# Gate weights in two passes, an own wait for the first x tile, and a changed order in a GLA/MLA/ConvGLU step

## The reference

```
h = rmsnorm(x, norm_mix[0])
q, k, v, r = split(h @ w_in)
log_a = log_sigmoid((h @ w_a1) @ w_a2 + b_a) / 16      # w_a1: 1024 x 16, w_a2: 16 x 512
b = cumsum(log_a) within a chunk
scores = sum_d q_i k_j exp(b_i - b_j), causal;  o = scores @ v + (q exp(b)) @ S
S_new = exp(b_last) S + (k exp(b_last - b))^T @ v       # S: the recurrent state, 128 x 256
o = rmsnorm(o) * silu(r);  x = x + o @ w_out
```

## Time and profile before

| | us |
|---|---|
| median of 3 runs | 2765.77 |
| lowest, highest | 2765.39, 2768.36 |
| profiled execution, its own time | 2768.41 |
| its span | 2766.6 |
| PE busy | 2708.2 (98%) |
| DVE busy | 1146.8 (41%) |
| ACT busy | 900.4 (33%) |
| POOL busy | 769.3 (28%) |

### The profile page before, as it was taken

One profiled execution on the slowest core, in us unless ns is written; L12 is line 12 of the kernel. 1 busy time (PEld: TensorE's weight loads), 2 busy tenths in 40 slices (PEclk: granted clock), 3 DMA queues, 4 the chain that ended last, 5 costly groups with the idle time before them and its releaser, 6 DMA issues.

```text
span 2766.6 us, 41263 instructions
## 1 busy us (share of the span) xinstructions
PE 2708.2 (98%) x17210; PEld 2607.8 (94%) x17210; DVE 1146.8 (41%) x2182; ACT 900.4 (33%) x1605; POOL 769.3 (28%) x324
## 2 busy tenths in 40 slices
PE   8999999999999999999999999999999999999999
PEld 6899999999999999999988888888999999999998
DVE  6634344463333333333624336556733333333324
ACT  7333242451111111112546666444521111111121
POOL 4121221262222222223512113322432222222221
PEclk9999999999999999999999999999999999999999
DMA  3110101011111111111213352212011111111112
GB/s 105 36 37 31 48 20 49 20 46 46 47 46 46 46 46 46 46 46 46 72 58 110 113 197 96 82 52 70 16 46 46 46 46 46 46 46 46 46 47 80
DMA packets 156507, 156.81 MB, mean 57 GB/s; under 512 B 15122, under 2 KB 137632, under 8 KB 156208
## 3 DMA queue, kind: packets, MB, share of 16 engines
q1 hardware_dynamic: 153935, 152.20, 17.2%
q10 hardware_dynamic: 2400, 2.10, 0.2%
HBM read 128.12 MB, written 26.15 MB: 56 GB/s over the span
## 4 chain that ended last, share of the span: by engine, by line
PE 90%; DVE 5%; ACT 2%; issue 2%; DMA 1%; SPq 0%; POOL 0%; DVEq 0%; ACTq 0%; POOLq 0%
PE ps L303 25%; PE ps L305 24%; PE ps L304 24%; PE ps L1864 2%; PE ps L852 2%; PE ps L1577 2%; PE ps L839 1%; PE ps L1848 1%; PE ps L840 1%; PE ps L841 1%; DVE xT L530 1%; DVE aP L2007 1%; DVE fa L716 1%; PE ps L923 1%; ACT aP L1950 1%
## 5 line engine op out<-in xcount | busy, mean ns | idle before, releaser
L303 PE MATMUL ps<-hh,whi 128*128 128x352 f32 x2664 | 864.5, 325 | 0.7 <-DVE hl L437 0.4
L304 PE MATMUL ps<-hl,whi 128*128 128x352 f32 x2664 | 854.8, 321 | 0.0
L305 PE MATMUL ps<-hh,wlo 128*128 128x352 f32 x2664 | 854.5, 321 | 0.0
L268 POOL TENSOR_TENSOR wlo<-wraw,whi 128x2048 fp32r<-128x2048 f32 (+1 forms) x79 | 361.5, 4575 | 660.9 <-ACT whi L261 631.6
L303 PEld LDWEIGHTS ps<-hh,whi 128*128 128x128 f32 x2664 | 500.6, 188 | 3.6 <-issue 1.3
L304 PEld LDWEIGHTS ps<-hl,whi 128*128 128x128 f32 x2664 | 501.3, 188 | 1.1 <-issue 0.2
L305 PEld LDWEIGHTS ps<-hh,wlo 128*128 128x128 f32 x2664 | 499.8, 188 | 0.0
L530 DVE TENSOR_TENSOR xT<-xT,ps 128x352 f32<-128x352 f32 x720 | 371.8, 520 | 261.9 <-PE ps L305 260.8
L303 PE MATMUL ps<-fahi,whi 128*128 128x352 f32 x1056 | 343.2, 325 | 2.6
L261 ACT ACTIVATE whi<-wraw 128x2048 fp32r<-128x2048 f32 x82 | 157.1, 1916 | 579.1 <-DMA wraw<-w_ffn_in 458.2
L305 PE MATMUL ps<-fahi,wlo 128*128 128x352 f32 x1056 | 341.2, 323 | 0.0
(11 more groups left out here) (301 smaller groups left out, 4091.4 us busy)
## 6 DMA issues: line engine op xcount, KB each, us to landing
wraw<-w_ffn_in SPq DMA_DIRECT2D x88, 512.0 KB, 4.9
wraw<-w_ffn_out SPq DMA_DIRECT2D x44, 512.0 KB, 4.1
wraw<-w_gla_in SPq DMA_DIRECT2D x24, 512.0 KB, 4.5
s_k<-kw SPq DMA_DIRECT2D x8, 784.0 KB, 3.3
akraw<-s_k SPq DMA_DIRECT2D x8, 784.0 KB, 4.2
s_v<-vst SPq DMA_DIRECT2D x8, 768.0 KB, 4.4
av<-s_v SPq DMA_DIRECT2D x8, 768.0 KB, 4.1
aqraw<-s_q SPq DMA_DIRECT2D x8, 528.0 KB, 5.8
```

The costliest lines, as they stand in the source:

```text
L268: pool.tensor_tensor(lo[:, 0:cols], raw[:, 0:cols], hi[:, 0:cols].bitcast(F32), ALU.subtract).then_inc(S("w_lo"), 1)
L303: nc.tensor.matmul(out, w[0], x[0], start=start, stop=False)
L304: nc.tensor.matmul(out, w[0], x[1], start=False, stop=False)
L305: return nc.tensor.matmul(out, w[1], x[0], start=False, stop=stop)
```

## The change

- The first x tile (tile 0) counts on the semaphore `consts`, together with the identity and the ones matrix. TensorE waits for it alone, then for tiles 1 and 2, then for 3 to 5, then for 6 to 8.
- TensorE turns tiles 4 and 5 behind the sums of chunk 0 instead of ahead of them.
- The gate weights w_a1 lie in one tile `a1p` of 48 columns per row tile: hi, zeros, lo. Per row tile there are two matmuls instead of three: all 48 columns by the hi activations, 16 columns by the lo ones. The part from lo weights comes out on partitions 32 to 47; ACT copies it to a sixth used block of `zs` (now 112 partitions), and `zah` gets a fourth copy of w_a2.
- At the first head, v unit 0 waits for 8 of the 12 minima; the other 4 are waited for behind it. ACT's last q/k copy comes ahead of the first decays. DVE does the minima of chunk 2 ahead of a scan. POOL clears `gkd` instead of DVE, for head 0.
- POOL splits the chunk for r (`gc(h, 2)`) in eight pieces of 256 columns instead of four of 512, in all heads.
- The output products wait for each state where it is first read, instead of for all nine ahead of the first.

```diff
@@ split_parts, pe_gla_t
-        def split_parts(who, c, parts=range(4)):
+        def split_parts(who, c, parts=range(4), n_parts=4):
...
-                cols = slice(q * WC // 4, (q + 1) * WC // 4)
+                cols = slice(q * WC // n_parts, (q + 1) * WC // n_parts)
...
-            wv = views((a1hi, a1lo), 0, KD, GRANK)
             for k in range(KD):
                 row_ready(pe, 0, j, k)
-                last = mm3(ps[0:GRANK, B_BANKS[j], 0:TC], [v[:, k, :] for v in wv],
-                           (hh[:, k, tc(j)], hl[:, k, tc(j)]), k == 0, k == KD - 1)
+                if k:
+                    pe.matmul(ps[0:GRANK, B_BANKS[j], 0:TC], a1p[:, k, 0:GRANK], hl[:, k, tc(j)], start=False, stop=False)
+                last = pe.matmul(ps[0:3 * GRANK, B_BANKS[j], 0:TC], a1p[:, k, :], hh[:, k, tc(j)],
+                                 start=(k == 0), stop=(k == KD - 1))
+                if k == 0:
+                    pe.matmul(ps[0:GRANK, B_BANKS[j], 0:TC], a1p[:, k, 0:GRANK], hl[:, k, tc(j)], start=False, stop=False)
             last.then_inc(S("t_mm"), 1)
@@ pe_gla_head
-                    pe.wait_ge(S("z_min"), NCH * GH)
+                    pe.wait_ge(S("z_min"), 2 * GH)
...
             pe.wait_ge(S("qk_sb"), h * 6 + 6)
+            pe.wait_ge(S("z_min"), NCH * GH)
...
-            pe.wait_ge(S("state"), h * 9 + 9)
             pe.wait_ge(S("qb"), h + 1)
...
                     if g > 0:
+                        if r_ < 3:
+                            pe.wait_ge(S("state"), h * 9 + g)
@@ t_copy (ACT)
-                for r_ in (0, 4):
-                    last = act.activation(zs[r_ * GRANK:(r_ + 1) * GRANK, tc(j)], ps[0:GRANK, B_BANKS[j], 0:TC], ACT.Copy)
+                for r_ in (0, 4, 6):
+                    t0 = 2 * GRANK if r_ == 6 else 0
+                    last = act.activation(zs[r_ * GRANK:(r_ + 1) * GRANK, tc(j)], ps[t0:t0 + GRANK, B_BANKS[j], 0:TC], ACT.Copy)
@@ act_gla_start
+            act_gla_qk(act, 6, 1, 2)
             act_gla_decays(act, 0, 0)
-            act_gla_qk(act, 6, 1, 2)
@@ dve_gla
-            z_scan(1, 0)
             for h in range(GH):
                 z_min(2, h)
+            z_scan(1, 0)
...
-            dve.wait_ge(S("z_log"), NCH * GH)
-            dve.memset(gkd[:, :], 0.0).then_inc(S("kd_zero"), 1)
@@ pool_gla_head, pool_gla
-            split_parts(pool, gc(h, 2))
+            split_parts(pool, gc(h, 2), range(8), 8)
...
             pool_split(pool, gc(0, 1), WC)
+            pool.wait_ge(S("z_log"), NCH * GH)
+            pool.memset(gkd[:, :], 0.0).then_inc(S("kd_zero"), 1)
@@ tensor: x_turn and the order
-                if t % 3 == 0:
-                    pe.wait_ge(S(f"x_loaded{t // 3}"), 3 * 16)
+                if t in (0, 1, 3, 6):
+                    pe.wait_ge(S(x_loaded(t)), 3 * 16 if t != 1 else 2 * 16)
...
-            for t in range(6):
+            for t in range(4):
                 x_turn(t)
             pe.wait_ge(S("mix_loaded"), 16)
             pe.transpose(ps[:, 3, 0:2 * KD], pmix[:, :], ident[0:2 * KD, 0:2 * KD]).then_inc(S("par_mm"), 1)
             x_sums_paired(pe, 0)
+            for t in range(4, 6):
+                x_turn(t)
```

More of the change, by code:

```diff
@@ L136, in build @@
         a1raw = at("a1raw", [P, KD * GRANK], R + 8 * T + 19 * DV + 4 * T)
-        a1lo = at("a1lo", [P, KD * GRANK], R + 8 * T + 19 * DV + 4 * T, F32R)
-        a1hi = at("a1hi", [P, KD * GRANK], R + 8 * T + 19 * DV + 4 * T + KD * GRANK, F32R)
-        A1 = (a1hi, a1raw, a1lo)
+        a1p = at("a1p", [P, KD, 3 * GRANK], R + 8 * T + 19 * DV + 4 * T + KD * GRANK, F32R)
         gq = at("gq", [P, 2, T], R)
@@ L155, in build @@
         gb = at("gb", [P, GH, T], R + 8 * T + 19 * DV)
-        ZK = 5 * GRANK
+        ZK = 7 * GRANK
         za = at("za", [ZK, GH * DK], R + 9 * D + 4 * P)
@@ L275, in split_parts @@
             for q in parts:
-                cols = slice(q * WC // 4, (q + 1) * WC // 4)
+                cols = slice(q * WC // n_parts, (q + 1) * WC // n_parts)
                 last = who.tensor_tensor(wlo[slot][:, cols], wraw[slot][:, cols],
                                          whi[slot][:, cols].bitcast(F32), ALU.subtract)
-            if 3 in parts:
+            if n_parts - 1 in parts:
                 last.then_inc(S("w_lo"), 1)
@@ L1354, in pool_gla @@
             x_pairs(0)
-            pool_split(pool, chunk(0), KD * GRANK, A1)
+            pool.wait_ge(S("w_hi"), 1)
+            pool.tensor_tensor(a1p[:, :, 2 * GRANK:3 * GRANK], a1raw[:, :].rearrange("p (k n) -> p k n", k=KD),
+                               a1p[:, :, 0:GRANK].bitcast(F32), ALU.subtract).then_inc(S("w_lo"), 1)
             pool_split(pool, gc(0, 0), WC)
@@ L2378, in x_square, with x_loaded @@
             return (sq0a, sq0b)[k // 4][:, k % 4, :]
+        def x_loaded(t):
+            return "consts" if t == 0 else f"x_loaded{t // 3}"
         def x_last():
@@ L2422, in x_load @@
                     src = A["x_prompt"][0, t0:t0 + n, :] if t < NG else A["x_sample"][0]
-                    sp.dma_start(xs[0:n, t, :], src).then_inc(S(f"x_loaded{t // 3}"), 16)
+                    sp.dma_start(xs[0:n, t, :], src).then_inc(S(x_loaded(t)), 16)
             x_load(range(3))
@@ L2502, in _ @@
             act.wait_ge(S("prow_zero"), 1)
-            for r_ in (0, 2, 4):
+            for r_ in (0, 2, 4, 6):
                 act.dma_start(za[r_ * GRANK:(r_ + 1) * GRANK, :], A["w_gla_a2"][0]).then_inc(S("consts_late"), 16)
@@ L2509, in _ @@
             x_squares(act, 0, range(KD))
-            act_split(act, chunk(0), KD * GRANK, A1)
+            act.wait_ge(S("w_loaded0"), 32)
+            act.wait_ge(S("prow_zero"), 2)
+            act.activation(a1p[:, :, 0:GRANK], a1raw[:, :].rearrange("p (k n) -> p k n", k=KD), ACT.Copy)\
+               .then_inc(S("w_hi"), 1)
             act_split(act, chunk(1), WC)
@@ L2516, in _ @@
             x_root_act(act, 1)
-            act.wait_ge(S("consts_late"), 16 * 5)
+            act.wait_ge(S("consts_late"), 16 * 6)
             act.activation(zah[:, :], za[:, :], ACT.Copy).then_inc(S("za_sb"), 1)
@@ L2533, in _ @@
             dve.memset(za[:, :], 0.0).then_inc(S("prow_zero"), 1)
+            dve.memset(a1p[:, :, GRANK:2 * GRANK].bitcast(F32), 0.0)
             dve.memset(prow[:, :, :], 0.0).then_inc(S("prow_zero"), 1)
```

## The result

| | before | after |
|---|---|---|
| median of 11 runs each | 2765.66 | 2773.66 |
| lowest, highest | 2764.24, 2768.36 | 2767.92, 2776.93 |
| profiled execution, its span | 2768.41, 2766.6 | 2772.24, 2770.4 |

The changed kernel is slower: ratio 1.0024 (6.6 us), 95% interval 1.0017 to 1.0032; the two medians are 8.0 us apart. I had forecast 2765.0 and a range up to 2768.8. Of these 3.8, 3.2 have arisen by the out projection of head 3, at the end of the part that the change touches.

The account below looks back on a forecast made before the run. TensorE, busy in 98% of the span, was taken as the bound, except in the start-up (0 to 79 us). Terms +0.7 + 0.8 - 2.3 = -0.8 us took the median 2765.77 to 2765.0; 8-in-10 range 2759.5 to 2768.8.

Parts of the forecast that it names:

- term 1: Start-up to the first level of head 0: all edits there together make it start 0.7 us later.
- Turned order, d = 1.5: Start-up, tiles 4 and 5 behind the sums: chain through norm and DVE returns to TensorE d = 1.5 us later.
- Gates in two passes, "None of the gain reaches the end": Gate matmuls in start-up: 1.3 us saved a chunk, 3.9 on TensorE, none reaching the end; third ACT copy +1.26.
- First head's order, +1.1 on DVE: Ahead of the first level: TensorE's 1.9 us wait goes; clearing gkd on POOL makes DVE's chain 1.1 us later.
- Term 2: Split in eight, levels 3 and 4 of four heads: more turns between DVE and POOL cost +0.8 us.
- Term 3: States where read, outputs of four heads: the 0.57 us wait goes in each, -2.3 us.
- The turned order is dear: Rival, chance 0.12: tiles 4 and 5 turned at the slow pace, d = 3, sum +0.7, 2766.5 us.
- The clock: Rival, chance 0.15: TensorE's falls to 1.2 GHz, 1.5 us each; both go, 2762.0, or two more, 2768.0.
- all of these come together: Whole kernel: slower by over 0.2% (over 2771.3 us), needing several bounds at once; chance 0.04.

Follow-up runs that it names:

- e3: Kernel before with one edit: output products wait for each state where it is read; 2762.72 us, ratio 0.9989.
- g2: Kernel before with one edit: POOL splits the weight chunk of level 3 in eight pieces instead of four; 2763.80 us, ratio 0.9996.
- g1: Changed kernel without tile 0's own wait and the turned order, POOL's chunk 1 lo pieces behind DVE's, v unit 0 waiting for all 12 minima; 2760.57 us.
- e2: Changed kernel with both x edits undone (tile 0's own wait, tiles 4 and 5 behind the sums); 2770.60 us, ratio 1.0016.
- f1: Changed kernel with both x edits undone, and POOL waits for DVE's four lo pieces of chunk 1 before its own; 2763.55 us, ratio 0.9990.
- e4: Kernel before with the two x edits alone (tile 0's own wait, tiles 4 and 5 behind the sums); 2770.04 us, ratio 1.0016.
- f3: Changed kernel with tiles 4 and 5 ahead of the sums again and v unit 0 waiting for all 12 minima; 2763.62 us, ratio 0.9993.
- f4: Kernel before with the gate weights in two passes alone; 2771.54 us, ratio 1.0018.
- h2: Changed kernel with POOL's lo pieces of chunk 1 behind DVE's and v unit 0 waiting for all 12 minima; 2766.79 us, ratio 1.0006.
- h4: Kernel before with one wait more: POOL's lo pieces of chunk 1 behind DVE's; 2766.81 us, ratio 1.0009.

## Why the prediction was wrong

By its own terms, in medians. The step that failed is term 1, and in it above all that the earlier t of the two passes would end in a wait and start nothing.

- **Term 1 (+0.7, bounds -0.8 and +2.2)** failed. It came out at about +12.5 (+10.8 by the ratios of the changed kernel, e3 and g2): the 13.1 us between g1 and the changed kernel, less 0.6 that g1 has below the two gaining edits (5.1 against 2.6 + 1.9). Undone one behind the other, they are 3.1 for the x edits (after to e2), 7.0 for POOL first (e2 to f1) and 3.0 for v unit 0 (f1 to g1). The traces of g1 and of the changed kernel are 8.4 apart at the out projection; the rest of the 13.1 they do not show.
  - *Turned order, d = 1.5.* The mechanism was right, the size off: d was 3.3, and 2.4 in e4. I let the last pair end at 16.4, as if the whole earlier start would reach it, and the last sum at 17.1. In e4, at full clock, the pair ended at 17.38 and tiles 4 and 5 were turned from 18.13. In the changed kernel the last sum ended near 19, as tile 3 took 1.78 and the first four sums 2.29, where I had 1.0 and 1.3. I had taken the fast pace of the earlier trace rows at 13.41, but there TensorE had idled 1.4 us and here 2.4, and the granted clock fell to 0.59. The own wait, which I priced at nothing, lengthens that idle time by starting and ending the first turns earlier.
  - *Gates in two passes, "None of the gain reaches the end".* That was true: the waits that I forecast came, 1.59 us at 34.46 and 1.10 at z of chunk 1, and 48 weight columns took 0.16 us a matmul like 16 (49.41, 49.57, 49.73 us), as I had assumed. But I asked only what the gain is worth, not what it would start. It released ACT earlier, ACT released POOL, and POOL came to stand a quarter of a us ahead of DVE. DVE's four then took 4.61 us instead of 1.83, and z of heads 2 and 3 came 2.8 us later. The earlier trace rows had shown what contention of the two costs; that they start 0.05 us apart at the lo pieces I did not treat as a race.
  - *First head's order, +1.1 on DVE.* The handover of `gkd` took 1.17 us of wait (DVE L1178), near my 1.09. But I took TensorE's removed wait of 1.9 us at L839 for a gain without price. It had kept the idle time in one place, ahead of work that had slack. Without it the first level ran at 1.2 GHz, 7.8 us to the second instead of 4.7.
- **Term 2 (+0.8, bounds -2.4 and +3)**: -1.9 in g2, not resolved, so probably wrong in sign, and within the bounds. The turns were much as played through: 0.98 becomes 0.57, and level 4 pays 0.20 in head 3 and 0.85 in head 0, where before had paid 0.90 as well. At full clock a head came out 0.07 us longer. That rarer clock falls outweigh this I had put into a rival, not into the term.
- **Term 3 (-2.3, bounds 0 and -3.9)**: right, -2.6 in e3 and 0.63 a head in its trace.
- **The rivals.** "The turned order is dear" named the right place and d = 3, but by its sum of 2766.5 it would have ended inside the noise. "The clock" had 1.5 us for each fall and two new ones, at 31 and 51 us; the falls came at 14 and 85, and that at 85 lasted over 6 us and cost 3.1. That all of these come together I gave 0.04.

## What to carry to other kernels

When a step is made shorter and its own gain is lost in a wait, follow what it releases: list for each shared resource which engine now arrives first, and do not build on a margin of a few tenths of a us: here 0.3 us turned the order round. Pin such an order with a wait where one engine is on the path and the other is not; here that gave 4 to 7 us where POOL had been first, and cost nothing that the times resolve where it had not. Two more lessons are smaller. Idle time of TensorE that could not be removed cost less in one piece, ahead of work that had slack, than spread ahead of the stage that all wait for. And a single profiled execution can sit nearly 4 us off its kernel's median, as g1's did, so compare stages in traces and whole times in medians of many runs.

## What the runs showed of the hardware

- Two engines with four lo pieces each (128x352, fp32): DVE first, 1.83 us for DVE; POOL first, 4.61. Back-to-back DVE instructions keep POOL out; back-to-back POOL instructions let DVE in between.
- TensorE's clock fell to 1.2 GHz behind idle time of 2.4 to 2.9 us (at 14 us in the changed kernel, at 43 to 45 in e2, f3 and f4, at 74 in f3), and also at 85 in the changed kernel, where 3.3 busy of 5.0 and 2.0 busy of 5.0 us went ahead. It did not always: behind the same 2.8 us idle the changed kernel at 45.9 stayed at full clock:

```profile
43.00:45.80 2.80, 0.10 (x1) 1.00 0.00 0
45.90:50.00 4.10, 4.10 (x17) 1.00 0.00 0
```

- What stays open: how often each kernel's executions have POOL first, and how often the clock falls at each place, since each kernel has one trace; what the x edits cost in the changed kernel (6.2 us by the medians of g1 and h2, 3.0 at the out projection in their traces; 3.1 by the medians of e2 and the changed kernel, 0.4 in theirs, where e2's clock fell at 44 and 109 us as well); why f3, with POOL first in its trace, has the median of f1, where POOL is held back; and what of h4's 1.5 us is real.
